# Five Strassen-type units instead of four in the steady feed-forward chunks, and the residual added by transfers

## The reference

```python
h2 = _rmsnorm(x, ffn_norm[l])
ff = jax.nn.silu(jnp.einsum('bsd,df->bsf', h2, w_gate[l])) * jnp.einsum('bsd,df->bsf', h2, w_up[l])
x = x + jnp.einsum('bsf,fd->bsd', ff, w_down[l])
```

## Time and profile before

| | us |
|---|---|
| median of 3 runs | 2172.93 |
| lowest, highest | 2172.77, 2174.07 |
| the profiled execution, its own time | 2175.64 |
| its span, first to last instruction | 2172.3 |
| weight loads in all | 400.9 MB, 56.2% of the 16 DMA engines' span |
| 16 of the 18 steady chunks | 63.5 each |

### The profile page before, as it was taken

One profiled execution on the slowest core, in us unless ns is written; L12 is line 12 of the kernel. 1 busy time (PEld: TensorE's weight loads), 2 busy tenths in 40 slices (PEclk: granted clock), 3 DMA queues, 4 the chain that ended last, 5 costly groups with the idle time before them and its releaser, 6 DMA issues.

```text
span 2172.3 us, 27182 instructions
## 1 busy us (share of the span) xinstructions
PE 2159.1 (99%) x10826; PEld 1843.7 (85%) x10826; DVE 1715.9 (79%) x1939; ACT 1083.0 (50%) x1145; POOL 22.2 (1%) x24
## 2 busy tenths in 40 slices
PE   9999999999999999999999999999999999999998
PEld 8899988888888888888888999888888888888886
DVE  5676774788899888889755866747888898888887
ACT  6454543554554455445443645445554454445544
POOL 0000000000000000000000000000000000000000
PEclk9999999999999999999999999999999999999999
DMA  7543455556556665665554434555565655665664
GB/s 265 179 137 117 148 173 194 178 198 205 194 195 197 201 198 196 204 198 194 194 189 158 151 113 158 173 178 192 194 197 198 203 193 194 198 207 194 198 206 158
DMA packets 221679, 402.77 MB, mean 185 GB/s; under 512 B 13440, under 2 KB 53664, under 8 KB 221472
## 3 DMA queue, kind: packets, MB, share of 16 engines
q1 hardware_dynamic: 220880, 400.90, 56.2%
q10 hardware_dynamic: 720, 0.78, 0.1%
HBM read 399.54 MB, written 2.10 MB: 185 GB/s over the span
## 4 chain that ended last, share of the span: by engine, by line
PE 95%; DVE 2%; DMA 1%; issue 1%; ACT 1%; SPq 0%; DVEq 0%; POOLq 0%; POOL 0%; ACTq 0%
PE bank L1021 19%; PE bank L1023 19%; PE bank L1022 19%; PE bank L698 10%; PE bank L700 10%; PE bank L699 10%; PE bank L658 3%; PE bank L823 1%; DMA stage<-in_w_down 1%; PE bank L764 0%; PE bank L887 0%; DMA stage<-in_w_in 0%; DVE w_lo L1551 0%; PE bank L875 0%; PE bank L765 0%
## 5 line engine op out<-in xcount | busy, mean ns | idle before, releaser
L1551 DVE TENSOR_TENSOR w_lo<-stage,w_hi 128x2048 fp32r<-128x2048 f32 (+4 forms) x318 | 678.0, 2134 | 266.7 <-ACT w_hi L1185 266.4
L1185 ACT ACTIVATE w_hi<-stage 128x2048 fp32r<-128x2048 f32 (+4 forms) x318 | 567.4, 1786 | 384.4 <-DMA stage<-in_w_down 191.3
L698 PE MATMUL bank<-w_hi,xt_hi 128*128 128x512 f32 (+4 forms) x1048 | 375.9, 359 | 2.0 <-DVE w_lo L1551 2.0
L700 PE MATMUL bank<-w_hi,xt_lo 128*128 128x512 f32 (+4 forms) x1048 | 368.9, 352 | 0.0
L699 PE MATMUL bank<-w_lo,xt_hi 128*128 128x512 f32 (+4 forms) x1048 | 368.7, 352 | 0.0
L1021 PE MATMUL bank<-w_hi,xt_hi 128*128 128x512 f32 x812 | 316.7, 390 | 0.5 <-DVE resid L2077 0.3
L1023 PE MATMUL bank<-w_hi,xt_lo 128*128 128x512 f32 x812 | 316.0, 389 | 0.0
L1022 PE MATMUL bank<-w_lo,xt_hi 128*128 128x512 f32 x812 | 315.9, 389 | 0.0
L1021 PE MATMUL bank<-w_hi,f_hi 128*128 128x512 f32 x696 | 271.3, 390 | 0.4 <-DVE f_lo L1966 0.4
L1023 PE MATMUL bank<-w_hi,f_lo 128*128 128x512 f32 x696 | 270.9, 389 | 0.0
L1022 PE MATMUL bank<-w_lo,f_hi 128*128 128x512 f32 x696 | 270.8, 389 | 0.0
(11 more groups left out here) (258 smaller groups left out, 2827.9 us busy)
## 6 DMA issues: line engine op xcount, KB each, us to landing
stage<-in_w_gate SPq DMA_DIRECT2D x176, 512.0 KB, 3.8
stage<-in_w_up SPq DMA_DIRECT2D x176, 512.0 KB, 4.7
stage<-in_w_down SPq DMA_DIRECT2D x174, 512.0 KB, 4.5
stage<-in_w_in SPq DMA_DIRECT2D x96, 384.0 KB, 3.7
stage<-in_w_out SPq DMA_DIRECT2D x64, 512.0 KB, 4.4
stage<-in_w_in SPq DMA_DIRECT2D x54, 512.0 KB, 4.5
stage<-in_w_in SPq DMA_DIRECT2D x16, 320.0 KB, 3.5
stage<-in_w_q_b SPq DMA_DIRECT2D x12, 384.0 KB, 3.8
```

The lines of the kernel that those rows point to most:

```text
L698: pe.matmul(acc, a, wh[:, i, :], start=first and i == 0, stop=False)
L700: mm = pe.matmul(acc, b, wh[:, i, :], start=False, stop=last and i == len(kts) - 1)
L1185: act.activation(w_hi[s][:, 0:kts * cols], stage[s][:, 0:kts * cols], ACT.Copy).then_inc(hi_made[s], 1)
L1551: vec.tensor_tensor(w_lo[s][:, 0:kts * cols], stage[s][:, 0:kts * cols], w_hi[s][:, 0:kts * cols].bitcast(F32), ALU.subtract).then_inc(lo_ ...
```

## The change

- The steady chunks (2 to 10) have five sets, units 0, 2, 3, 5 and 6, and three pairs, 1, 4 and 7. The second chunk still has three sets. The row tiles are paired at a distance of five instead of four, and the token sums grow from four to five blocks of each kind. The buffers are laid out anew.
- VectorE no longer adds the down banks of chunks 0 to 9 to the residual. ScalarE copies each bank into one of six buffers `part_sum` (`copy_out`), and GpSimd issues a transfer from there onto `resid` with addition (`add_part`), 128 x 512 values each, eight a chunk. Column groups 0 and 3 share two of the six buffers. TensorE waits for the copies (`part_out`) where it waited for the adds; ScalarE waits for the last transfer out of a buffer before it fills it again; VectorE waits for all of them once at the end of each layer's chunks, before the last adds.
- ScalarE signals the rounding of a set's fourth block by itself (`fourth_hi_made`), and VectorE's subtraction for that block waits for this signal instead of the one behind the sums.

```diff
-SETS = (0, 3, 4, 6)
-PAIRS = (1, 2, 5, 7)
+SETS = (0, 2, 3, 5, 6)
+PAIRS = (1, 4, 7)
...
-SECOND_TILES = (8, 9), (10, 11), (12, 13), (3, 7), (14, 15)
+SECOND_TILES = (10, 11), (12, 13), (8, 9), (3, 4), (14, 15)
...
+        part_sum = [arena(f"part_sum{i}", [P, NCH], F32, at * SEQ) for i, at in enumerate((8, 10, 12, 14, 82, 84))]
...
 def added(f, n):
-                    pe.wait_ge(x_added, layer * X_ADDS + 2 * ADDS + f * ADDS + n)
+                    pe.wait_ge(part_out, layer * COPIES + f * ADDS + n)
...
                     act.wait_ge(sums_made, layer * N_SETS + set_index(n) + 1 + sets)
-                    act.activation(w_hi[s][:, 3 * NCH:], stage[s][:, 3 * NCH:], ACT.Copy)
+                    act.activation(w_hi[s][:, 3 * NCH:], stage[s][:, 3 * NCH:], ACT.Copy).then_inc(fourth_hi_made, 1)
...
+                def copy_out(c, n0, chunk, turn=0):
+                    n = n0 + c
+                    act.wait_ge(used[n % 4], layer * QUADS + n // 4 + 2 + turn)
+                    for t in range(NT):
+                        i = PART_OF[c] + t
+                        if layer or n0 != U_SECOND + 8 or c == 3:
+                            twice = 2 if c in (0, 3) else 1
+                            act.wait_ge(part_added[i], 16 * twice * (layer * (FF_CHUNKS - 1) + chunk) + c // 3 * 16)
+                        act.activation(part_sum[i][:, :], bank[DOWN_BANKS[c][t]][:, :], ACT.Copy).then_inc(part_out, 1)
...
                     for c in range(4):
                         if c == 0 and after_set:
                             silus(f + 1)
-                        prepare(n0 + c + LEAD, turn, sets,
-                                (lambda: ff_turn(f + 1, TURN_BANKS, 0)) if c == 3 else None)
+                        if c:
+                            copy_out(c - 1, n0, f, turn)
+                        if c == 3:
+                            copy_out(3, n0, f, turn)
+                            ff_turn(f + 1, TURN_BANKS, 0)
+                        prepare(n0 + c + LEAD, turn, sets)
...
+                def add_part(f, c):
+                    for t in range(NT):
+                        i = PART_OF[c] + t
+                        pool.wait_ge(part_out, layer * COPIES + f * ADDS + NT * c + t + 1)
+                        pool.dma_start(resid[:, t, c * NCH:(c + 1) * NCH], part_sum[i][:, :], accum_op=ALU.add)\
+                            .then_inc(part_added[i], 16)
+                for f in range(FF_CHUNKS - 1):
+                    for c in range(4):
+                        add_part(f, c)
...
-                    vec.wait_ge(hi_made[s], made(quad, n))
+                    vec.wait_ge(fourth_hi_made, k + 1)
                     vec.tensor_tensor(w_lo[s][:, 3 * NCH:], stage[s][:, 3 * NCH:], w_hi[s][:, 3 * NCH:].bitcast(F32),
                                       ALU.subtract)
+                    vec.wait_ge(hi_made[s], made(quad, n))
...
-                            add_down(c - 1, n0, turn)
-                        prepare(n0 + c + LEAD, turn, sets, between if c == 3 else None)
+                        prepare(n0 + c + LEAD, turn, sets,
+                                (lambda: ff_turn(f + 1, TURN_BANKS, 0)) if c == 3 else None)
...
-                vec.wait_ge(x_added, layer * X_ADDS + X_ADDS)
+                for i in range(6):
+                    vec.wait_ge(part_added[i], (32 if i < 2 else 16) * (layer + 1) * (FF_CHUNKS - 1))
```

More of the change, by code:

```diff
@@ L77 @@
 ADDS = NT * (D_MODEL // NCH)
-X_ADDS = ADDS * (1 + FF_CHUNKS)
+X_ADDS = 2 * ADDS
+COPIES = ADDS * (FF_CHUNKS - 1)
+PART_OF = 0, 2, 4, 0
 QUADS = UNITS // 4
@@ L339, in program @@
         xn = arena("xn", [P, NT, D_MODEL], F32, 16 * SEQ)
-        f_hi = [arena(f"f_hi{i}", [P, 4, SEQ], F32R, 4 * SEQ * (2 * i)) for i in range(2)]
-        f_lo = [arena(f"f_lo{i}", [P, 4, SEQ], F32R, 4 * SEQ * (2 * i + 1)) for i in range(2)]
+        f_hi = [arena(f"f_hi{i}", [P, 4, SEQ], F32R, 46 * SEQ * i) for i in range(2)]
+        f_lo = [arena(f"f_lo{i}", [P, 4, SEQ], F32R, 4 * SEQ + 46 * SEQ * i) for i in range(2)]
+        part_sum = [arena(f"part_sum{i}", [P, NCH], F32, at * SEQ) for i, at in enumerate((8, 10, 12, 14, 82, 84))]
         xs_hi = arena("xs_hi", [P, 4, K_SET, P], F32R, 16 * SEQ)
[L344 to L350, removed]
+        xs_lo = arena("xs_lo", [P, 4, K_SET, P], F32R, 26 * SEQ)
+        xs = arena("xs", [P, 4, K_SET, P], F32, 26 * SEQ)
+        kept = [arena(f"kept{i}", [P, NCH], F32, 36 * SEQ + NCH * i) for i in range(5)]
+        sums = [arena(f"sums{i}", [P, 3, NCH], F32, 46 * SEQ + 3 * NCH * i) for i in range(3)]
+        sums_lo = [arena(f"sums_lo{i}", [P, 3, NCH], F32R, 46 * SEQ + 3 * NCH * i) for i in range(3)]
+        sums_hi = [arena(f"sums_hi{i}", [P, 3, NCH], F32R, 64 * SEQ + 3 * NCH * i) for i in range(3)]
+        x_whole = arena("x_whole", [P, 2 * K_SET, SEQ], F32, 64 * SEQ)
         stage_x = arena("stage_x", [P, 4 * NCH], F32, 60 * SEQ)
@@ L421, in program @@
         down_made = sem("down_made")
+        part_out = sem("part_out")
+        part_added = [sem(f"part_added{i}") for i in range(6)]
         ms_made, rstd_made = sem("ms_made"), sem("rstd_made")
@@ L437, in program @@
         xs_raw, xs_hi_made, xs_made = sem("xs_raw"), sem("xs_hi_made"), sem("xs_made")
+        fourth_hi_made = sem("fourth_hi_made")
         sum_chain, sums_made, raw_hi_made = sem("sum_chain"), sem("sums_made"), sem("raw_hi_made")
@@ L593, in load_sets @@
                         for w, at in ((w_gate, 0), (w_up, 2)):
-                            if in_set(n) or n0 == U_SECOND and i == 5:
-                                m = 3 if not in_set(n) else sets_of(n).index(i)
+                            if in_set(n):
+                                m = sets_of(n).index(i)
                                 src = w[layer, m * P:(m + 2 * K_SET) * P, bass.ds(f * NCH, NCH)]\
@@ L1141, in last_down @@
                         if not last and t == 1 and c >= 2:
-                            added(f, 4)
+                            need(x_added, X_ADDS, 2 * ADDS + 4)
                             norm_turn("norm1", range(2 * c - 4, 2 * c - 2), layer + 1)
@@ L1481, in _ @@
                         silus(FF_CHUNKS - 1)
+                    else:
+                        copy_out(c - 1, U_PEEL + 8, FF_CHUNKS - 2)
                     if c == 1 and layer == DEPTH - 1:
@@ L1487, in _ @@
                         ff_turn(FF_CHUNKS - 1, TURN_BANKS, 1)
+                copy_out(3, U_PEEL + 8, FF_CHUNKS - 2)
                 if layer < DEPTH - 1:
@@ L2070, in gate_up_sets @@
                             ff_turn(0, TURN_BANKS, 0)
-                def add_down(c, n0, turn=0):
-                    n = n0 + c
-                    vec.wait_ge(used[n % 4], layer * QUADS + n // 4 + 2 + turn)
-                    for t in range(NT):
-                        part = resid[:, t, c * NCH:(c + 1) * NCH]
-                        vec.tensor_tensor(part, bank[DOWN_BANKS[c][t]][:, :], part, ALU.add).then_inc(x_added, 1)
                 def down(f, n0, turn=0, sets=0, after_set=True):
-                    def between():
-                        add_down(3, n0, turn)
-                        ff_turn(f + 1, TURN_BANKS, 0)
                     for c in range(4):
```

4 lines of the change are left out of this document (removed).

## The result

The changed kernel takes 2201.12 us (median of 4 runs, 2198.65 to 2202.56), beside 2173.46 for the kernel before (4 runs, 2172.77 to 2174.07). The ratio is 1.0125, with a 95% interval of 1.0113 to 1.0137: 27.7 us slower. The forecast was 2187 with a range of 2160 to 2206: the sign and the range held, the change was forecast at half of what came.

The account below looks back on a forecast made before the run. The prediction took TensorE's instructions as the bound (busy 2159.1 of 2172.3 us). Its terms, -12.2 + 27.0 - 0.4 = +14.4 us on a median of 2172.93, gave 2187 us, range 2160 to 2206.

Parts of the forecast that it names:

- small things: Longer mixed-token operations (1.8 us, mostly in gaps) and f_lo no longer behind two adds at layer ends: -0.4 us together.
- Part 1: Steady chunks: one pair becomes a fifth set, 54 matmuls fewer, 12.2 us removed; a VectorE set falls from 7.02 to 6.74.
- Parts 2 and 3: Residual adds moved off VectorE, and the order around a chunk's start: without disturbance all 12.2 us are kept.
- Part 4: Chunk start: group 1's two adding transfers delay unit 2's load, costing 18 x (1.9 - 0.4) = 27.0 us.
- The warning that the spare is gone if a set stays at 7.0 us: Before set 6: the spare 0.4 us would vanish and TensorE stand even without transfers, by four more gaps of 0.28.
- L: Lateness in microseconds of unit 2's load at a chunk's start, caused by adding transfers; taken as 1.9.
- Each microsecond beyond 0.4 is paid in full: At each chunk's start, lateness of unit 2's load above set 6's 0.4 us to spare stops TensorE equally, 18 times.
- The middle of two bounds: Lateness of unit 2's load: 1.1 us if transfer bytes count once, 2.7 if twice; 1.9 was taken.
- Other loads meet transfers too, and have room: Loads besides unit 2's cost nothing: unit 3's has 2.5 us, unit 1's 0.5 on ScalarE and more on VectorE.
- The end-of-layer waits: VectorE's wait for all six parts delays its last adds by a few us; TensorE needs them 16 later: nothing.
- The other side: Transfers miss unit 2's load or cost little: TensorE stands at most 0.4 us a chunk, 2160 to 2168 us; chance 0.33.
- Rival 4: Slow adding transfers make ScalarE wait for parts before group 3's copies; at 8 us each, 54 us more; chance 0.03.

Follow-up runs that it names:

- without transfers: Changed kernel without its adding transfers: ScalarE's copies stay, the down products of chunks 0 to 9 are never added to the residual; 2163.86 us.
- two groups: Changed kernel with the adding transfers of column groups 0 and 1 only; groups 2 and 3 are copied but not added; 2193.45 us.
- half-size: Changed kernel with each of the 160 adding transfers cut to 256 of its 512 columns; 2179.78 us.
- ScalarE-queue: Changed kernel with plain copies instead of adding transfers, issued by ScalarE behind its copies, not by GpSimd; 2181.03 us.
- plain transfers: Changed kernel with the same eight GpSimd transfers a chunk as plain copies, the addition left out; 2201.26 us.
- With act_sb first: Changed kernel with adding transfers one at a time behind chosen units, a seventh buffer, and act_sb ahead of xs_lo; 2181.02 us, against 2183.75 without that order.
- the version with late adds: Changed kernel without transfers; VectorE adds ScalarE's copies, two ahead of unit 1, six in the next chunk ahead of units 8 and 9; act_sb first; 2161.02 us.
- VectorE's adds in their old place: Changed kernel with five sets and the fourth block's signal, but VectorE adds the residual as before, no copies or transfers; 2200.53 us.

## Why the prediction was right or wrong

The kernels before, without transfers, with two groups and changed put a measured number beside each term:

| term | forecast | measured |
|---|---|---|
| the set, the signal, small things | -12.2 - 0.4 | 2163.86 - 2173.46 = -9.6 |
| group 1's transfers against unit 2's load (measured with group 0's) | +27.0 | 2193.45 - 2163.86 = +29.6 |
| all other transfers | 0 | 2201.12 - 2193.45 = +7.7 |
| sum | +14.4 | +27.7 |

The second and third measured numbers can each be off by some 3 us, since the runs of the two-group kernel spread over 8. The sum was 13.3 us short: 3.0 in the first term, 2.6 in the second, and 7.7 in the third, which the prediction put at nothing.

**Part 1, right.** Without transfers a chunk takes 62.80 us, as the prediction had it, and the set is 6.65 us, forecast 6.74.

**Parts 2 and 3, right.** The plan around the chunk's start holds in the kernel without transfers. Set 6 had 0.65 us to spare, not 0.4; the shorter sets account for it. The warning that the spare is gone if a set stays at 7.0 us was right too, and cheaply put: it costs the whole gain.

**Part 4, the size right, the reason wrong.** L was taken as 1.9 and is 1.91. "Each microsecond beyond 0.4 is paid in full" is confirmed to 0.05 us by four kernels: 62.80 + L - 0.4 gives 63.69, 63.75, 64.28 and 64.70 for the half-size, ScalarE-queue, two-group and plain transfers, and they have 63.69, 63.79, 64.26 and 64.68. But the place isn't the one of the sum: the 0.4 was set 6's, f_lo was given 0.5, and TensorE stands on f_lo, while set 6 had 0.65. That the two spares were so close is luck. And L was worked out from engine time (0.8 or 1.6 us each), and engine time doesn't set it: 0.69 us each made the load 2.30 late, 0.72 from the other queue 1.35, 1.55 made it 1.91. The middle of two bounds fell on the right value by luck.
On the rule of the Trainium skill cited there (Collectives: The Full Stack, "The bandwidth ceiling: the fold count and why AG ≠ RS ≠ AR"): the page states it for the reduce step of a ring of cores. Here the engine time agrees, 1.55 us against 0.69, and the time of the kernel doesn't follow it, 2201.12 against 2201.26.
The two queues differ by 20 us for the same bytes. The Trainium skill says (DMA: Bandwidth & Descriptors, "Issuing engines are not separate DMA queues") that transfers run on the same 16 engines and interleave whichever engine started them, and that issuing from several engines saves only the sequencer's time. The 20 us don't agree with that, as far as packets and moments allow the comparison.

**The count, a little low.** Part 4 paid 18 times. The last chunk interval of each layer, 57.70 and 57.75 us without transfers, takes 60.62 and 61.68 with two groups: 2.9 and 3.9 more, where 1.5 was counted each time. Of this 1.3 and 1.6 us are the stand at the chunk's start, as counted. The rest is a place that the prediction doesn't have: behind the last f_hi of a layer no set follows, and ScalarE rounds a down unit ahead of f_hi. That unit's load is late too (ScalarE in the two-group kernel; 2.56 us of idle time without transfers), and TensorE stands on f_lo a 19th and a 20th time:

```profile
1066.79 1.92 ACT L1191 ACTIVATE w_hi<-stage 128x2048 fp32r<-128x2048 f32 x1 [3.97 <-DMA stage<-in_w_down]
1068.61 1.06 ACT L1419 ACTIVATE f_hi<-bank 128x512 fp32r<-128x512 f32 x2
...
1072.29 0.50 PE L1027 MATMUL bank<-w_hi,f_hi 128*128 128x512 f32 x1 [0.60 <-DVE f_lo L2005]
```

From matmul to matmul these two cost 0.8 and 1.6 us, most of the 2.6 between 27.0 and 29.6.

**"Other loads meet transfers too, and have room": wrong,** and the largest miss. This term was put at nothing, and groups 2 and 3 cost 7.7 us, of which some 1.6 are the clock (next paragraph). Unit 3's load was given 2.5 us of room. In the kernel without transfers its first sum stands 7.7 us after its issue, waiting for VectorE, so the room is real; the delay was never worked out. With all transfers its first sum comes 10.0 to 11.4 us after the issue in 7 of 18 chunks, and 9.0 to 9.9 in the others. The eight-transfer and the two-group kernel agree to 0.3 us over the first layer's eight intervals (514.78 and 514.49) and differ by 6.0 in the second's (519.70 and 513.74). The excess is in four chunks there, with unit 3's first sum 10.4 to 11.2 us after its issue in all four. One was shown above; another has 1.6 us of clock. The interval at the end of that layer has 1.9 more (63.57 against 61.68), with unit 3's first sum at 11.4 and TensorE on set 3.

**The clock, not in the sum at all.** The chunk of 66.67 us, in TensorE's timeline:

```profile
1847.33 0.78 PE L1027 MATMUL bank<-w_hi,xt_hi 128*128 128x512 f32 x1 [1.96 <-DVE f_lo L2004]
1847.90 0.63 PE L1028 MATMUL bank<-w_lo,xt_hi 128*128 128x512 f32 x1
```

and the stretch that follows:

```profile
1847.20:1849.20 2.00, 1.87 (x5) 1.51 (x6) 2.00 (x3) 0.91 (x1) 0.00 (x0) 0.54 1.12 310
```

The load came 7.76 us after its issue. TensorE stood for two microseconds and came back at a granted clock of 0.5 (1.2 of 2.4 GHz), with matmuls 0.43 us apart instead of 0.227. By the rule the chunk would have taken 62.80 + 2.70 - 0.4 = 65.1; the clock added 1.6. The other seventeen chunk starts, with stands up to 1.65 us, show 1.00. The length of the stand alone doesn't decide it. Plain transfers, a chunk's start and the two microseconds behind it:

```profile
887.09 0.50 PE L1027 MATMUL bank<-w_hi,xt_hi 128*128 128x512 f32 x1 [2.55 <-DVE f_lo L2004]
887.10:889.10 2.00, 2.00 (x9) 1.66 (x10) 2.00 (x2) 1.49 (x2) 0.00 (x0) 1.00 0.02 7
```

The same with VectorE's adds in their old place:

```profile
563.44 0.50 PE L1025 MATMUL bank<-sums_hi,xt_hi 128*128 128x512 f32 x1 [1.62 <-DVE resid L2082]
564.90:566.90 2.00, 2.00 (x6) 1.54 (x6) 2.00 (x3) 0.70 (x1) 0.00 (x0) 0.50 0.00 0
```

A stand of 2.55 us left the clock at 1.00, and one of 1.62 with 0.22 behind it was followed by 0.50. What decides isn't shown.

**Small things, wrong sign.** The mixed tokens were put down in gaps, at -0.4 with f_lo. The longer xs_lo stands ahead of act_sb on VectorE, and TensorE waits for act_sb in both second chunks, 3.4 us in all. With act_sb first 2.7 of them came back. The step looked at gaps ahead of the first set and not at what is queued behind the operation that grows. The end-of-layer waits were right: VectorE stands 6.7 us there at most, and TensorE doesn't.

**The rivals.** The other side, no stand and 2160, would have needed transfers that miss the load; the version with late adds shows that this time was there, 2161, without them. Rival 4, ScalarE waiting for the parts, didn't come: its copies wait for TensorE alone, 34.4 us in all.

## What to carry to other kernels

Work moved off a full engine has to be priced where it lands: against each transfer whose landing is on the edge, and against what is queued behind each instruction that grows. Ask first whether the same engine has an idle place later on; here VectorE could do six of eight adds 30 us later, for nothing, while the transfers cost 37 us. A gain that rests on a few tenths of a microsecond of spare needs every such tenth: the fifth set and a wait of 0.3 us in each set were worth about the same 12 us.

## What the runs showed of the hardware that was not expected

- An adding transfer of 256 KB within SBUF takes 1.55 us of all 16 DMA engines, a plain one 0.69 to 0.72, a half-size adding one 0.87, and it lands 6.6, 5.3 (GpSimd) or 4.0 (ScalarE), and 5.1 us after its issue.
- What such transfers do to a load beside them doesn't follow their engine time. Two plain ones from GpSimd make it 2.30 us late, two from ScalarE's queue 1.35, two adding ones 1.9, two adding ones of half the size 1.29. What does set it is open.
- Three pairs issued within 6.5 us put a load at 11.8 us from issue to first use, where unit 2's takes 5.06 in the kernel without transfers.
- TensorE's clock fell to half behind one stand of 1.96 us and one of 1.62, and stayed at full behind one of 2.55.
